# Memory attention of two blocks: heads interleaved with the query tiles, PSUM banks numbered in that order

## The reference

```python
def mem_cross_attention(h, mem_n, w_q, w_kv, w_o):
    q = (h @ w_q).reshape(B, S, MEM_HEADS, MEM_HEAD_DIM)
    kv = (mem_n @ w_kv).reshape(B, M, 2, MEM_HEADS, MEM_HEAD_DIM)
    k, v = kv[:, :, 0], kv[:, :, 1]
    s = jnp.einsum('bqhd,bkhd->bhqk', q, k) * (MEM_HEAD_DIM ** -0.5)
    p = jax.nn.softmax(s, axis=-1)
    o = jnp.einsum('bhqk,bkhd->bqhd', p, v).reshape(B, S, D)
    return o @ w_o
```

## Time and profile before

| | us |
|---|---|
| median of 3 runs | 3675.81 (3674.46 to 3677.61) |
| profiled execution | 3675.11 |
| its span, first to last instruction | 3673.3 |
| PE busy | 3267.4 (89%) |
| DVE, ACT, POOL busy | 1135.1, 1050.9, 710.9 |
| mean granted PE clock | 0.936 |
| attention of the first block, first scores to first matmul of `o` | 316.08 to 387.87 |
| the same of the second block | 1704.29 to 1774.28 |

### The profile page before, as it was taken

The page is one execution under the profiler, slowest core; times in us unless marked ns, Lnnn a source line. Parts: engine busy times, 40 slices in busy tenths (PEclk is TensorE's granted clock), DMA queues, the critical chain, the costliest instruction groups (busy, mean ns, idle before and its releaser), DMA issues.

```text
span 3673.3 us, 38880 instructions
## 1 busy us (share of the span) xinstructions
PE 3267.4 (89%) x16196; PEld 2261.4 (62%) x16196; DVE 1135.1 (31%) x1830; ACT 1050.9 (29%) x1795; POOL 710.9 (19%) x344
## 2 busy tenths in 40 slices
PE   7998899997867888897899999889899989999996
PEld 5676678874546888665678875456685664333332
DVE  4433320224286555443320213385131120000001
ACT  3533332325323222133432421234321131111110
POOL 3122244431210000022234430000242221000001
PEclk9998999998888888999999999999999999999998
DMA  3231152420200000221122323110122239989996
GB/s 114 85 126 46 46 183 92 147 89 29 73 19 1 2 2 2 81 98 58 46 92 92 94 90 96 57 35 1 58 75 78 78 140 378 388 355 387 386 387 276
DMA packets 217629, 448.05 MB, mean 122 GB/s; under 512 B 14176, under 2 KB 191360, under 8 KB 204528
## 3 DMA queue, kind: packets, MB, share of 16 engines
q1 hardware_dynamic: 197664, 389.04, 29.1%
q10 hardware_dynamic: 9744, 36.18, 2.4%
q0 software_dynamic: 10048, 20.35, 1.6%
HBM read 502.14 MB, written 31.46 MB: 145 GB/s over the span
## 4 chain that ended last, share of the span: by engine, by line
PE 76%; DVE 8%; DMA 8%; ACT 4%; issue 2%; POOL 1%; SPq 0%; ACTq 0%; POOLq 0%; DVEq 0%
PE product_banks L563 13%; PE product_banks L564 13%; PE product_banks L565 12%; PE product_banks L535 8%; PE product_banks L1923 5%; PE product_banks L1960 4%; DMA A<-in_w_down 4%; DMA A<-in_w_up 3%; PE product_banks L627 3%; PE product_banks L1125 1%; PE score_banks L1106 1%; PE product_banks L1342 1%; PE product_banks L2397 1%; PE product_banks L586 1%; PE stat_bank L749 1%
## 5 line engine op out<-in xcount | busy, mean ns | idle before, releaser
L472 POOL TENSOR_TENSOR Wr_parts<-Wr,Wr_parts 128x1024 fp32r<-128x1024 f32 x186 | 447.2, 2406 | 1427.1 <-ACT Wr_parts L449 1427.1
L564 PE MATMUL product_banks<-A_parts,Wr_parts 128*128 128x512 f32 x1408 | 558.7, 397 | 0.0
L449 ACT ACTIVATE Wr_parts<-Wr 128x1024 fp32r<-128x1024 f32 x186 | 195.9, 1058 | 728.7 <-PE product_banks L565 635.2
L1923 PE MATMUL product_banks<-A,Wr 128*64 128x512 f32 x1504 | 344.3, 600 | 13.9 <-DMA A<-in_w_up 12.8
L563 PE MATMUL product_banks<-H_parts,Wr_parts 128*128 128x512 f32 x728 | 297.7, 409 | 24.4 <-POOL Wr_parts L472 20.8
L564 PEld LDWEIGHTS product_banks<-A_parts,Wr_parts 128*128 128x128 f32 x1408 | 269.3, 191 | 61.9 <-issue 2.2
L563 PE MATMUL product_banks<-A_parts,Wr_parts 128*128 128x512 f32 x680 | 269.2, 396 | 32.0 <-DVE A_parts L485 15.6
L565 PE MATMUL product_banks<-H_parts,Wr_parts 128*128 128x512 f32 x728 | 291.6, 401 | 0.0
L472 POOL TENSOR_TENSOR shared_con_parts<-Wr,shared_con_parts 128x1024 fp32r<-128x1024 f32 x80 | 193.2, 2415 | 435.4 <-ACT shared_con_parts L449 435.4
L565 PE MATMUL product_banks<-A_parts,Wr_parts 128*128 128x512 f32 x680 | 266.8, 392 | 0.0
L1923 PEld LDWEIGHTS product_banks<-A,Wr 128*64 128x64 f32 x1504 | 116.7, 138 | 218.4 <-issue 214.9
(11 more groups left out here) (447 smaller groups left out, 5175.0 us busy)
## 6 DMA issues: line engine op xcount, KB each, us to landing
A<-in_w_gate SPq DMA_DIRECT2D x32, 2048.0 KB, 14.1
A<-in_w_up SPq DMA_DIRECT2D x32, 2048.0 KB, 18.1
A<-in_w_down SPq DMA_DIRECT2D x32, 2048.0 KB, 13.5
Wr<-in_m_w_up SPq DMA_DIRECT2D x32, 1024.0 KB, 5.4
Wr<-in_m_w_down SPq DMA_DIRECT2D x32, 1024.0 KB, 4.7
Wr<-in_w_in SPq DMA_DIRECT2D x32, 1024.0 KB, 5.4
Wr<-in_c_w_kv SPq DMA_DIRECT2D x16, 1024.0 KB, 5.0
expert_rows<-LB ACTq DMA_DIRECT2D x12, 1024.0 KB, 4.3
```

The source lines that it names most:

```text
L449: nc.scalar.activation(weight_parts(s)[0], loaded_part(s), ACT.Copy).then_inc(*mark("weights_high", s))
L472: nc.gpsimd.tensor_tensor(lo, loaded_part(s), hi, ALU.subtract).then_inc(*mark("weights_split", s))
L564: pe.matmul(bank[:, :], hi[:, k, :], x_lo, start=False, stop=False)
L1923: mm = pe.matmul(BK[r, 0 if kind == "gate" else 1, :], XT[b % 2][:, k * P + CAP * h:k * P + CAP * h + CAP], unit_rows((kind, b, h))[:, k, ...
```

## The change

The work of each head stays what it was; its place in the queues of PE, ScalarE and VectorE changes, and with it the numbering of the banks. In both attentions, PE now runs: q3, scores 0, q4, scores 1, q5, turns 0, q6, value products 0, scores 2, turns 1, q7, turns 2, scores 3, value products 1, value products 2, turns 3, value products 3, output product. ScalarE and VectorE get the matching order. The helpers are cut in two for this: `mix_pe` into `probs_turn_pe` and `mix_pe`, `turned_act` into `turned_act` and `mixed_act`, `softmax_dve` into `softmax_max_dve` and `softmax_norm_dve`. In the list of tiles the two value tiles of head 0 move ahead of q7, and `turn_of` gives each tile's place in that list, from which its bank and the tile it waits for follow. Tag `c` keeps its order through the new helpers.

```diff
--- before.py
+++ after.py
@@ -374,6 +374,12 @@
                 L.chunks, L.tiles = [], L.cols // P
             tiles += [(L.evac, (L.name, j)) for j in range(L.tiles)]
             nchunk += len(L.chunks)
+        for tag in ("a0", "a1_"):
+            if tag + "q" in by_name:
+                q0 = tile0[tag + "q"]
+                late, first = tiles[q0 + 7], tiles[q0 + 8:q0 + 10]
+                tiles[q0 + 7:q0 + 10] = first + [late]
+        turn_of = {key: g for g, (_, key) in enumerate(tiles)}
 
         def chunk_source(L, c):
             if L.kind == "gates":
@@ -503,14 +509,14 @@
 
         def bank_for(pe, name, j):
 
-            g = tile0[name] + j
+            g = turn_of[name, j]
             if g >= 4:
                 who, key = tiles[g - 4]
                 pe.wait_ge(*at("products_read_by_" + who, key))
             return banks[g % 4]
 
         def psum_of(name, j):
-            return banks[(tile0[name] + j) % 4]
+            return banks[turn_of[name, j] % 4]
 
         def slot_of(pe, name, n, kk, ww):
             g = chunk0[name] + n
@@ -1025,13 +1031,20 @@
                 take_product(act, tag + "q", j)
                 if j == SIDE - 1:
                     norm_root(act, tag + "n")
+                if j in (3, 4):
+                    softmax_act(act, tag, j - 3, scale)
+                if j == 5:
+                    turned_act(act, tag, 0, dt)
                 if j == 6:
-                    softmax_act(act, tag, 0, scale)
-            softmax_act(act, tag, 1, scale)
-            for h in range(heads):
-                turned_act(act, tag, h, dt)
-                if h + 2 < heads:
-                    softmax_act(act, tag, h + 2, scale)
+                    mixed_act(act, tag, 0, dt)
+                    softmax_act(act, tag, 2, scale)
+                    turned_act(act, tag, 1, dt)
+            turned_act(act, tag, 2, dt)
+            softmax_act(act, tag, 3, scale)
+            for h in (1, 2):
+                mixed_act(act, tag, h, dt)
+            turned_act(act, tag, 3, dt)
+            mixed_act(act, tag, 3, dt)
             for j in range(8):
                 ps = take_product(act, tag + "o", j, ahead=(j < 7))
                 branch_square(act, tag + "x", j, ps[:, :])
@@ -1067,6 +1080,8 @@
                     act.wait_ge(*at("products_done", (tag + "ov", (h - 1) * dt - 1)))
                 nc.scalar.activation(turned(h, m), (B6 if m == 0 else B7)[:, :], ACT.Copy).then_inc(
                     *mark("turned_ready", (tag, h, m)))
+
+        def mixed_act(act, tag, h, dt):
             for d in range(dt):
                 j = h * dt + d
                 if dt == 2:
@@ -1078,17 +1093,25 @@
                     *mark("products_read_by_act", (tag + "ov", j)))
 
         def attend_pe(pe, tag, heads, dt):
-            def early_scores(t):
-
-                if t in (4, 6):
-                    scores_pe(pe, tag, t // 2 - 2, dt)
-
-            product(pe, tag + "q", hn_parts_attn, low_ready(tag + "n"), then=early_scores,
+            def between(t):
+
+                if t in (3, 4):
+                    scores_pe(pe, tag, t - 3, dt)
+                if t == 5:
+                    probs_turn_pe(pe, tag, 0)
+                if t == 6:
+                    mix_pe(pe, tag, 0, dt)
+                    scores_pe(pe, tag, 2, dt)
+                    probs_turn_pe(pe, tag, 1)
+
+            product(pe, tag + "q", hn_parts_attn, low_ready(tag + "n"), then=between,
                     early=(tag + "n", arena(8)))
-            for h in range(heads):
-                mix_pe(pe, tag, h, dt)
-                if h + 2 < heads:
-                    scores_pe(pe, tag, h + 2, dt)
+            probs_turn_pe(pe, tag, 2)
+            scores_pe(pe, tag, 3, dt)
+            mix_pe(pe, tag, 1, dt)
+            mix_pe(pe, tag, 2, dt)
+            probs_turn_pe(pe, tag, 3)
+            mix_pe(pe, tag, 3, dt)
             product(pe, tag + "o", parts(24, 0),
                     lambda k: [("products_read_by_dve", (tag + "ov", k))])
             branch_sum(pe, tag + "x")
@@ -1107,7 +1130,7 @@
                                    key_tile(tag, h * dt + d), start=(d == 0), stop=(d == dt - 1))
             mm.then_inc(*mark("scores_ready", (tag, h)))
 
-        def mix_pe(pe, tag, h, dt):
+        def probs_turn_pe(pe, tag, h):
             pe.wait_ge(*at("probs_normed", (tag, h)))
             pe.wait_ge(*at("products_read_by_act", (tag + "v", by_name[tag + "v"].tiles - 1)))
             for m in range(MT):
@@ -1117,6 +1140,8 @@
                     mm = pe.transpose((B6 if m == 0 else B7)[:, q * P:(q + 1) * P],
                                       probs(h)[:, q, m * P:(m + 1) * P], ident)
                 mm.then_inc(*mark("probs_turned", (tag, h, m)))
+
+        def mix_pe(pe, tag, h, dt):
             for d in range(dt):
                 j = h * dt + d
                 bank = bank_for(pe, tag + "ov", j)
@@ -1126,12 +1151,15 @@
                                    start=(m == 0), stop=(m == MT - 1))
                 mm.then_inc(*mark("products_done", (tag + "ov", j)))
 
-        def softmax_dve(dve, tag, h, scale):
-            m0, d0 = 32 + 4 * (h % 2), 40 + 4 * (h % 2)
+        def softmax_max_dve(dve, tag, h, scale):
+            m0 = 32 + 4 * (h % 2)
             dve.wait_ge(*at("scores_ready", (tag, h)))
             link(dve, nc.vector.tensor_reduce(small[:, m0:m0 + 4], scores, AX_X, ALU.max))
             nc.vector.tensor_scalar(small[:, m0:m0 + 4], small[:, m0:m0 + 4], -scale, None,
                                     ALU.mult).then_inc(*mark("row_max_ready", (tag, h)))
+
+        def softmax_norm_dve(dve, tag, h):
+            d0 = 40 + 4 * (h % 2)
             dve.wait_ge(*at("probs_ready", (tag, h, TT - 1)))
             link(dve, nc.vector.reciprocal(small[:, d0:d0 + 4], small[:, d0:d0 + 4]))
             for q in range(TT):
@@ -1139,23 +1167,31 @@
                                               small[:, d0 + q:d0 + q + 1], None, ALU.mult)
             ins.then_inc(*mark("probs_normed", (tag, h)))
 
+        def mixed_low_dve(dve, tag, h):
+            for j in (2 * h, 2 * h + 1):
+                dve.wait_ge(*at("high_part_ready", (tag + "ov", j)))
+                nc.vector.tensor_tensor(high(j), psum_of(tag + "ov", j)[:, :], high(24 + j),
+                                        ALU.subtract).then_inc(
+                    *mark("products_read_by_dve", (tag + "ov", j)))
+
         def attend_dve(dve, i, tag):
             norm_rstd(dve, tag + "n")
             for j in range(8):
                 ps = await_product(dve, tag + "q", j)
                 nc.vector.tensor_tensor(tile(16 + j), ps[:, :], RS[:, :], ALU.mult).then_inc(
                     *mark("products_read_by_dve", (tag + "q", j)))
-                if j == 5:
-                    softmax_dve(dve, tag, 0, 1.0 / 16)
+                if j in (3, 4):
+                    softmax_max_dve(dve, tag, j - 3, 1.0 / 16)
+                    softmax_norm_dve(dve, tag, j - 3)
+                if j == 6:
+                    mixed_low_dve(dve, tag, 0)
+                    softmax_max_dve(dve, tag, 2, 1.0 / 16)
+                    softmax_norm_dve(dve, tag, 2)
             deferred(tag + "n", ("products_read_by_dve", (tag + "q", 7)))
-            for h in range(6):
-                if 0 < h < 4:
-                    softmax_dve(dve, tag, h, 1.0 / 16)
-                for j in range(2 * h - 4, 2 * h - 2) if h >= 2 else ():
-                    dve.wait_ge(*at("high_part_ready", (tag + "ov", j)))
-                    nc.vector.tensor_tensor(high(j), psum_of(tag + "ov", j)[:, :], high(24 + j),
-                                            ALU.subtract).then_inc(
-                        *mark("products_read_by_dve", (tag + "ov", j)))
+            softmax_max_dve(dve, tag, 3, 1.0 / 16)
+            softmax_norm_dve(dve, tag, 3)
+            for h in (1, 2, 3):
+                mixed_low_dve(dve, tag, h)
             for t in range(1, DT - 1):
                 branch_add(dve, tag + "x", t)
             norm_add_parts(dve, tag + "x", arena(40),
@@ -1432,7 +1468,9 @@
                 softmax_act(act, "c", h, P ** -0.5)
                 if h:
                     turned_act(act, "c", h - 1, 1)
+                    mixed_act(act, "c", h - 1, 1)
             turned_act(act, "c", 3, 1)
+            mixed_act(act, "c", 3, 1)
 
             def take_va(j):
                 ps = take_product(act, "va", j)
@@ -1486,6 +1524,7 @@
                 if h < 4:
                     scores_pe(pe, "c", h, 1)
                 if h:
+                    probs_turn_pe(pe, "c", h - 1)
                     mix_pe(pe, "c", h - 1, 1)
             product_rows(pe, "va", lambda k, m: hn(k)[:, m * P:(m + 1) * P], lambda k: [],
                          then=lambda t: hnorm_pe(pe, 8, t, t))
@@ -1516,7 +1555,8 @@
             nc.vector.memset(small[:, 254:255], 0.0).then_inc(*mark("residual_free", 0))
             hnorm_dve(dve, 0, 8)
             for h in range(4):
```

(3 more changed lines are left out.)

## The result

The changed kernel takes 3627.56 us (median of 4 runs, 3624.25 to 3633.09) against 3676.71 (3674.46 to 3678.77): ratio 0.9868, 95% interval 0.9851 to 0.9885. That is 49.1 us less; 3631 was forecast, with 3625 to 3643 as the range. A second measurement of the same two kernels gave 3628.14 against 3674.88, ratio 0.9878 (0.9861 to 0.9894).

A forecast was written before the change was run, and what follows sets the result against it. PE's idles on each head's chain and the half clock behind them bound both attentions; stretches of 71.79 and 69.99 us, each to become 48.6, save 44.6 together, so 3675.11 falls to 3630.5, median 3631, range 3625 to 3643.

The forecast's parts named there:

- The five idles and their clock: PE's waits before head 1's scores and four value products, 16.58 us, plus 6.71 of half clock, in the first block's attention.
- the value products, put at 4 x 3.51: In the attention stretch's sum, PE's value products of each of the four heads cost 3.51 us start to start.
- The layout: First block's new PE order step by step: 48.6 us without q4, slacks 1.4 for head 2, 2.0 for head 3.
- The one uncovered wait: PE idle between head 3's turns and the last value products, about 0.4 us, the same as before.
- The clock: PE's granted clock in the attention stretches, 0.88 and 0.93 before, was to be 1.00 with the idles gone.
- Costs put at nothing: Table load (1.28 us) hidden in ScalarE's wait, POOL missing every row maximum, and the extra changeovers: no cost in the attention.
- the 1.6 put as the most: A collision of POOL's split with VectorE's row maximum scaling costs up to 1.6 us, mostly absorbed by slacks.
- The bank order: Banks follow issue order, so q7 waits for q5's read, not q3's; that read is 14 us old.
- The uncovered tail: Rival: heads 2 and 3 fall late, up to 9.8 us per attention, total 3640 to 3651; chance 0.13.
- The clock did not fall in the interleaved stretch: Rival denied here: alternating tiles and matmuls bring half clock, slower, total up to 3727; chance 0.02.
- Nothing was given back: Rival denied here: a later transfer or queue fixed in time returns up to all, 3650 to 3676; chance 0.05.
- more than I count, shorter warm-ups by luck: Rival: full clock also at first output tiles, or shorter warm-ups later by luck, 3620 to 3626; chance 0.03.

The follow-up runs named there:

- e5: Changed kernel with head 2's row maximum taken three times in both attentions, 2.5 us later; 3628.97 us in one profiled execution.
- e3: Against the kernel before, only scores and softmax of heads 0 and 1 moved behind q3 and q4, banks by the plan; 3646.79 us, ratio 0.9926.
- e7: Changed kernel with POOL's split of q6 held until head 0's scores are done, to collide with VectorE's scaling; 3626.73 us in one profiled execution.
- e4: Changed kernel with the old numbering of the banks, queues in the new order; 3625.80 us, ratio 0.9869 to the kernel before.
- e6: Changed kernel with head 2's row maximum taken five times in both attentions, 5.0 us later; 3634.68 us in one profiled execution.
- e1: Changed kernel with the new order in the first block's attention only, the old in the second; 3650.32 us, ratio 0.9934 to the kernel before.
- e0: The changed kernel measured and profiled again, unchanged; 3628.14 us against 3674.88 for the kernel before.
- e2: Changed kernel with the new order in the second block's attention only, the old in the first; 3657.76 us in one profiled execution.
- e9: The kernel before, unchanged, profiled once more; 3683.68 us in one profiled execution.

## Why the prediction was right

**The five idles and their clock.** Right in kind and size: 45.7 us in the two stretches, 44.6 forecast. My sum for the stretch with q4 was 48.6 + 5.55 = 54.1, measured 53.6. The term that is off is the value products, put at 4 x 3.51. That is their cost ahead of turns; ahead of scores they took 3.43 (335.80 to 339.23), two heads in a row 6.87 (353.47 to 360.34), and ahead of the output product 3.11 (361.77 to 364.88), as they had before the change (384.76 to 387.87). That is 0.6 less; turns with a tile behind them took 6.46 in place of 6.43 (342.68 to 349.14), scores with one 9.05 in place of 9.00.

**The layout.** Head 1's scores were laid out 9.00 us after head 0's and came 9.05 after; head 2's turns 37.8 after and came so; the output product 54.1 after, and came 53.6 after. Slacks: 1.4 forecast for head 2, 1.47 read, and some 1.5 by e5; 2.0 for head 3, 1.88 read.

**The one uncovered wait** was 0.39 us, unchanged, as put.

**The clock.** In both blocks it came back whole, as put. One reason given was too simple, that half clock came only behind the idles longer than 0.39 us. The longer ones differ among themselves: of the two idles of 3.19 us one was followed by products of 5.37 us and the other by 3.67, and e3 shows the same.

**Costs put at nothing.** The table load went into the wait. POOL met no scaling step: five splits, from 312.72 on and each 1.4 us behind its tile as laid out, and 0.17 us for all heads. The nearest gap was 1.14 us (first split done at 312.72 + 2.35 = 315.07, scaling of head 0 at 316.21), where 1 was forecast. e7 shows a collision that cost 1.1 us and that head 0 hid; the 1.6 put as the most is the one in the earlier trace rows. The rule of the Trainium skill, "SBUF — State Buffer", section "SBUF: two separate sides", that the two share ports as a lock, agrees with e7's 1.29 us. The bank order was put down as harmless; e4 shows more, that it is also needless.

**The rivals.** The uncovered tail did not occur; e5 shows that it would have begun at a delay of 1.5 us, and e6 that one late head with 3.5 us of idle costs 6.6 and 5.4 us, over the 4.9 a head (3.19 and 1.70) that I had put. The clock did not fall in the interleaved stretch: granted 1.00 in both. So the oscillation that the Trainium skill, "TensorE: Matmul & The Clock Gate", section "A second HAM failure mode: psum-queue depth-cycling", describes is not seen with these groups. Nothing was given back: e1's 24.6 us in the total for 23.75 in the stretch.

**What the sum did not have.** The total can't be told to a few us from one profile: the middle is 1311 or 1321 us by the clock and the rest 1891 to 1900. The first profiles of the two kernels differ by 42.0, the medians by 49.1 and 46.7. My case "more than I count, shorter warm-ups by luck" had 3620 to 3626 at a chance of 0.03; three of the eight single executions of the changed kernel lie in it (they run from 3622.70 to 3633.09), while both medians lie inside the forecast's own 3626 to 3638. So what is borne out is the sum of the stretches, to 1.1 us; that the median came within 3.4 us of 3631 is in part luck, since neither the two courses of the clock in the middle nor the spread of the expert phase stood in the sum.

## What to carry to other kernels

When PE waits for a chain of short steps on other engines, lay the chain out step by step against the work that could stand in PE's queue meanwhile, and count the slack of each link; start-to-start times from the old profile carried that to half a microsecond in 54. An idle can cost more than itself: 3.5 us of it cost 5.4 to 6.6 (e6), 0.95 only 1.2 (e5), so it pays to break up the long ones first. It need not: one of the two idles of 3.19 us was followed by full clock. And read the gain in the stretch that was changed before reading it in the total, where another part of the kernel may vary by as much between executions.

## What the runs showed of the hardware that was not expected

- A stream of small matmuls can stay at half clock although PE is busy. The 465 matmuls in front of the RWKV output sums took 23.4 to 23.5 us at 0.93 where that was read (before, e0, e5, e6), or 34.0 at 0.60 with PE busy for 31.25 of them (changed, e2; e9 is alike), in different executions of one kernel. The idle in front was 2.08 to 2.30 us in all twelve. The clock had taken another course from some 300 us earlier; what decides there is open. That the change is neither needed nor enough is shown by e0, e2 and e9.
- ScalarE's table load did not wait for what its activation waited for: it started 3.76 us ahead of the exp, directly behind the weight part in front of it. In the kernel before, it ran directly ahead of the exp, from 332.03 to 333.31 with the exp at 333.32.
